# Sums of squares with the squares added on GpSimd and one ones-product on TensorE, at six places of a four-layer and expert kernel

## The chip, the core and the metric

The kernel runs on one core of a Trainium2 chip. The metric is the device time of one execution in microseconds. All arithmetic is float32. The engines are TensorE (PE in the profile, PEld for its weight loads), VectorE (DVE), ScalarE (ACT), GpSimd (POOL) and SyncE (SP), which here only issues the weight DMAs.

## What is computed

Four layers work on 256 latent tokens and 256 context tokens of 1024 features (kinds: windowed attention, low-rank attention, chunked mLSTM, windowed attention), and a further block with dilated attention, a delta rule and 32 routed experts works on the latent tokens. Around each layer's mixer stand two normalisations for each of the two token streams:

```python
def rmsnorm(x, g):
    y = xf * lax.rsqrt(jnp.mean(xf * xf, axis=-1, keepdims=True) + EPS)
    return (y * g.astype(jnp.float32)).astype(x.dtype)

h_l = rmsnorm(x_lat, g_pre) * (1.0 + sc_l[:, None, :]) + sh_l[:, None, :]
h_c = rmsnorm(x_ctx, g_pre) * (1.0 + sc_c) + sh_c
y_l, y_c = mixer(h_l, h_c, need_ctx=need_ctx)
x_lat = x_lat + gt_l[:, None, :] * rmsnorm(y_l, g_post)
if need_ctx:
    x_ctx = x_ctx + gt_c * rmsnorm(y_c, g_post)
```

The last layer (number 3) gives no context output. The sums over the 1024 features in these norms are what the change is about.

## The kernel before

Tokens lie along the free dimension and features across the 128 partitions, in KT = 8 tiles: XT holds the residual stream as 8 tiles of 512 tokens (256 latent, LATENT, then 256 context, CONTEXT), HT its normed form, YT the gated output of a mixer, SQ squares. A sum over features is a sum over 8 tiles and over partitions. `sum_squares` (L358) does both on TensorE: for each tile k it waits for the square and multiplies it by a 128x128 matrix of ones, all eight accumulating in one PSUM bank, which leaves the sum in every partition. `square` (L355) is the ScalarE square of one tile, `root` (L365) the ScalarE root of mean plus eps, `inverse` (L370) the VectorE reciprocal, `residual` (L374) the two VectorE operations per tile that scale YT and add it to XT.

The program is a row of blocks. In a block each engine runs its own list in order, engines are tied by semaphores, and at its end all engines meet at a barrier. The blocks that matter here alternate:

- `project_out` (L512), out-projection of a layer. TensorE makes 8 tiles for latent tokens (s = 0), then, in layers 0 to 2 (`beside`), 8 for context tokens (s = 1), each of 8 products of 256 columns into one of four PSUM banks. ScalarE squares each tile into SQ (L560) and copies it gated into YT (L561). VectorE adds the eight squares of the latent tiles into SQ tile 0 (`sum_tiles`, L580), and one ones-product (L528) gives the post-norm's sum. After context tile 0 comes the first root; VectorE then forms the reciprocal and the residual of the latent tokens; ScalarE squares the new residual after context tile 4; TensorE takes these squares with `sum_squares` after context tile 5, and ScalarE takes the second root after context tile 6. VectorE forms the reciprocal and then adds the squares of the context tiles (L580 again), which ends the block.
- The first block of the next layer (`window_layer` L805, `latent_layer` L912, `memory_layer` L1070). Its start is common: `first_tiles` on TensorE, `norm_scalar` on ScalarE, `norm_vector` on VectorE. TensorE makes a ones-product of the context tiles' added squares (L411), then the latent half of three tiles (j = 0, 1, 2), then `sum_squares` of the context tokens' new residual, then the latent half of tile 3 (in layers 1 and 2 also the context halves). Meanwhile ScalarE finishes the latent norm (L404), VectorE makes the context residual, 16 operations (L377, L378), and ScalarE squares each tile as it comes (L356). The sum's root and reciprocal release the context norm (L391, L404).

GpSimd is used in none of this: it runs a few memsets, one group of them in layer 2 after the context norm (L1126), and six masks of two inputs (L1908) in the later delta rule. Weights come in 2 MB chunks by DMA from SP's queue into three slots; a slot is refilled when TensorE has finished with it.

Of the kernel before, what the change touches and what calls it, by code (L numbers as in the profile page):

```python
# [14 lines left out]
KT = D // P  # L15
# [140 lines left out]
def layers_and_experts_kernel(nc, t, consts_at, out):  # L156
# [3 lines left out]
    with ctx:  # L160
# [103 lines left out]
        def modulation_chunks(l, a, b, name=None):  # L264
# [7 lines left out]
        dve_chain = Chain(ctx.enter_context(nc.semaphore("dve_chain")))  # L272
        act_chain = Chain(ctx.enter_context(nc.semaphore("act_chain")))
        pool_chain = Chain(ctx.enter_context(nc.semaphore("pool_chain")))
        names = ("vectors_loaded tokens_loaded consts_loaded late_loaded transposed transposed_taken cond_ready squares_ready "
                 "square_sum_ready rms_ready inverse_ready rstd_ready scaled_ready tile_ready tile_taken rope_mixed rope_taken "
                 "scores_ready max_ready exp_ready scores_used probs_ready probs_turned turned_copied heads_ready "
                 "heads_taken rows_copied columns_ready columns_taken h_ready normed_ready residual_ready a_ready b_ready c_ready d_ready e_ready f_ready g_ready i_ready j_ready k_ready").split()
# [2 lines left out]
        def at(name, n):  # L281
            return S[name].sem, S[name].at(n)
# [75 lines left out]
        def sum_squares(pe, tok, sums, sq):  # L358
# [3 lines left out]
                ins = nc.tensor.matmul(sums, ones, sq[:, k, tok], start=(k == 0), stop=(k == KT - 1))  # L362
            ins.then_inc(S["square_sum_ready"].sem, 1)

        def root(act, sums, tok, nth=0):  # L365

            act.wait_ge(*at("square_sum_ready", nth + 1))
            nc.scalar.activation(RMS[:, tok], sums, ACT.Sqrt, bias=const("eps"), scale=1.0 / D).then_inc(S["rms_ready"].sem, 1)
# [38 lines left out]
        def first_tiles(pe, pending, tiles, product):  # L407


            if pending:  # L410
                nc.tensor.matmul(PS[:, 6, 0:LAT], ones, SQ[:, 0, CONTEXT], start=True, stop=True).then_inc(  # L411
                    S["square_sum_ready"].sem, 1)
            for s, tok in enumerate((LATENT, CONTEXT)):
                for j, streams, done in tiles:
                    if pending and tok is LATENT and j == 3:
                        sum_squares(pe, CONTEXT, PS[:, 7, 0:LAT], SQ)
                    if s < streams:
                        for k in range(KT):
                            pe.wait_ge(*at("h_ready", s * KT + k + 1))
                            ins = product(j, k, tok)  # L420
                        if s == streams - 1:
                            ins.then_inc(done[0], 1)

        def norm_passed(streams, pending=False):
            S["normed_ready"].passed(KT * streams)
            S["h_ready"].passed(KT * streams)
            if pending:
                S["residual_ready"].passed(KT)
                S["squares_ready"].passed(KT)
                S["square_sum_ready"].passed(2)  # L430
                S["rms_ready"].passed(2)

# [79 lines left out]
        def project_out(l, ot, streams):  # L512

            first = ws.first[f"l{l}_w_out"]
            tiles = [(s, m) for s in range(streams) for m in range(KT)]
            done, n_plain = tile_signals([first + m // 4 if s == streams - 1 and m % 4 == 3 else None for s, m in tiles])
            beside = streams == 2
            with nc.Block() as block:

                @block.sync  # L520
                def _(sp):
                    ws.load_until(sp, first + 2)

                @block.tensor
                def _(pe):
                    def sum_tiles():
                        pe.wait_ge(*at("c_ready", 1))
                        nc.tensor.matmul(PS[:, 4, 0:LAT], ones, SQ[:, 0, LATENT], start=True, stop=True).then_inc(  # L528
                            S["square_sum_ready"].sem, 1)

                    for j, (s, m) in enumerate(tiles):
                        if s == 0 and m % 4 == 0:
                            ws.wait(pe, first + m // 4)
                        w = ws.view(first + m // 4)
                        if j >= 4:
                            pe.wait_ge(*at("tile_taken", j - 3))
                        for k in range(KT):
                            ins = nc.tensor.matmul(PS[:, j % 4, 0:LAT], w[:, k, (m % 4) * P:(m % 4 + 1) * P],  # L538
                                                   ot[:, k, s * LAT:(s + 1) * LAT], start=(k == 0), stop=(k == KT - 1))
                        ins.then_inc(done[j][0], 1)  # L540
                        if (s, m) == (1, 0):
                            sum_tiles()
                        if (s, m) == (1, 5):
                            sum_squares(pe, LATENT, PS[:, 5, 0:LAT], SQ)
                    if not beside:
                        sum_tiles()
                        sum_squares(pe, LATENT, PS[:, 5, 0:LAT], SQ)

                @block.scalar
                def _(act):  # L550
                    def squares():
                        for k in range(KT):
                            act.wait_ge(*at("residual_ready", k + 1))
                            square(act, k, LATENT, SQ)

                    act.wait_ge(*at("b_ready", 1))
                    for j, (s, m) in enumerate(tiles):
                        act.wait_ge(*done[j])
                        tok = slice(s * LAT, (s + 1) * LAT)
                        nc.scalar.activation(SQ[:, m, tok], PS[:, j % 4, 0:LAT], ACT.Square).then_inc(S["a_ready"].sem, 1)  # L560
                        nc.scalar.activation(YT[:, m, tok], PS[:, j % 4, 0:LAT], ACT.Copy, scale=GATE[:, m, s:s + 1]).then_inc(  # L561
                            S["tile_taken"].sem, 1)
                        if (s, m) == (1, 0):
                            root(act, PS[:, 4, 0:LAT], LATENT)
                        if (s, m) == (1, 4):
                            squares()
                        if (s, m) == (1, 6):
                            root(act, PS[:, 5, 0:LAT], LATENT, 1)
                    if not beside:
                        root(act, PS[:, 4, 0:LAT], LATENT)  # L570
                        squares()
                        root(act, PS[:, 5, 0:LAT], LATENT, 1)

                @block.vector
                def _(dve):
                    def sum_tiles(s):
                        tok = slice(s * LAT, (s + 1) * LAT)
                        for m in range(1, KT):
                            dve.wait_ge(*at("a_ready", s * KT + m + 1))
                            ins = nc.vector.tensor_tensor(SQ[:, 0, tok], SQ[:, 0, tok], SQ[:, m, tok], ALU.add)  # L580
                            if m < KT - 1:
                                dve_chain.link(dve, ins)
                        ins.then_inc(S["c_ready"].sem, 1)

                    nc.vector.tensor_tensor(GATE[:], modulation(l)[:, 2 * KT:3 * KT, :],
                                            col(f"l{l}_g_post").unsqueeze(2).to_broadcast([P, KT, 2]), ALU.mult).then_inc(S["b_ready"].sem, 1)
                    sum_tiles(0)
                    inverse(dve, LATENT)
                    dve.wait_ge(*at("tile_taken", KT))
                    residual(dve, LATENT)  # L590
                    inverse(dve, LATENT, 1)
                    if beside:
                        sum_tiles(1)

            S["tile_ready"].passed(n_plain)
            S["tile_taken"].passed(KT * streams)
            S["a_ready"].passed(KT * streams)
            S["b_ready"].passed(1)
            S["c_ready"].passed(streams)
            S["residual_ready"].passed(KT)  # L600
            S["squares_ready"].passed(KT)
            for n in ("square_sum_ready", "rms_ready"):
                S[n].passed(2)

# [200 lines left out]
        def window_layer(i, need_ctx):  # L805
# [17 lines left out]
            with nc.Block() as block:  # L823

                @block.sync
                def _(sp):
                    ws.load_until(sp, first + 5)

                @block.tensor
                def _(pe):  # L830
                    def rope(n):
# [80 lines left out]
        def latent_layer():  # L912
# [16 lines left out]
            with nc.Block() as block:  # L929

                @block.sync
                def _(sp):
                    ws.load_until(sp, c_ukv + 1)

                @block.tensor
                def _(pe):
# [133 lines left out]
        def memory_layer():  # L1070
# [46 lines left out]
            with nc.Block() as block:  # L1117

                @block.sync
                def _(sp):  # L1120
                    ws.load_until(sp, c_in + 7)

                @block.gpsimd
                def _(pool):
                    pool.wait_ge(*at("h_ready", 2 * KT))
                    nc.gpsimd.memset(raw[:, :, :, 0:2], 0.0)  # L1126
                    nc.gpsimd.memset(raw[:, :, :, LAT + 2:LAT + 4], 0.0).then_inc(S["a_ready"].sem, 1)
                    nc.gpsimd.memset(va[:, :, :, DV:DV + 1], 1.0)
# [1481 lines left out]
```

## Time and profile before

| | us |
|---|---|
| median of 3 runs | 2608.21 |
| lowest and highest | 2607.4, 2610.09 |
| span of the profiled execution | 2608.5 |
| TensorE busy in it | 2454.0 |
| VectorE busy | 921.2 |
| ScalarE busy | 640.1 |
| GpSimd busy | 15.1 |

The profiled execution has no device time of its own beside its span, which runs from its first to its last instruction; the span is 0.3 us over the median of the runs. Busy times of TensorE are modelled ends of pipelined products, so distances from start to start are used for it. A float32 product leaves two matmul records.

### The profile page before, as it was taken

Reading aid. Unit: us, or ns where it says so; the run is one execution under the profiler, and the core shown is the slowest. Engines: PE = TensorE matmul, PEld = TensorE weight load, DVE = VectorE, ACT = ScalarE, POOL = GpSimd, SP = SyncE. Lnnn points to the kernel's source line nnn. Section 1 sums busy time; section 2 is a strip of 40 time slices with the busy share of each in tenths; the row PEclk is TensorE's granted clock in tenths of the full one; section 3 lists DMA queues with packets and bytes.
Section 4 is the critical chain, followed back from the end, with each engine's and each line's share of the span. In section 5 each row is a group of like instructions: output and inputs, shape, how many; then the busy total and the mean of one; then the engine's idle time right before and its main releaser. Section 6 shows DMA issues by size and latency. Waiting matters only on the chain. (4 is left out here: it accounts for less than half of the span.)

```text
span 2608.5 us, 31940 instructions
## 1 busy us (share of the span) xinstructions
PE 2454.0 (94%) x12046; PEld 1314.0 (50%) x12047; DVE 921.2 (35%) x2118; ACT 640.1 (25%) x1479; POOL 15.1 (1%) x15
## 2 busy tenths in 40 slices
PE   6999999999999998899899789999999999999997
PEld 4546686457744567776686563333333233333222
DVE  2208523043510584427353433232232223233223
ACT  3116523232311253326332321111111111111111
POOL 0000000000000000000001000000000000000000
PEclk9999999999999998899899799999999999999999
DMA  7127920200211102238331048977999986999997
GB/s 291 65 83 273 348 93 33 81 32 1 97 65 36 63 1 76 95 120 316 137 130 65 31 187 347 415 287 293 407 418 418 418 334 270 417 418 418 418 418 296
DMA packets 154191, 568.02 MB, mean 218 GB/s; under 512 B 10800, under 2 KB 12336, under 8 KB 121040
## 3 DMA queue, kind: packets, MB, share of 16 engines
q1 hardware_dynamic: 154096, 566.72, 55.7%
q8 instruction: 63, 1.03, 0.2%
q14 instruction: 32, 0.26, 0.0%
HBM read 565.64 MB, written 1.05 MB: 217 GB/s over the span
## 5 line engine op out<-in xcount | busy, mean ns | idle before, releaser
L2335 PE MATMUL PS<-BIG,PW 128*64 128x512 f32 x2304 | 513.9, 599 | 16.7 <-DMA BIG<-in_w 16.6
L2335 PEld LDWEIGHTS PS<-BIG,PW 128*64 128x64 f32 x2304 | 159.7, 137 | 368.3 <-issue 315.9
L2359 PE MATMUL PS<-BIG,PW 128*64 128x512 f32 x1152 | 256.7, 598 | 8.6 <-ACT PW L2431 8.6
L2491 DVE TENSOR_SCALAR PW<-PS 128x512 f32<-128x512 f32 x36 | 24.9, 692 | 562.4 <-PE PS L2335 562.4
L2428 ACT ACTIVATE PW<-PW 128x512 f32<-128x512 f32 x36 | 22.7, 630 | 799.1 <-DVE PW L2491 799.1
L2359 PEld LDWEIGHTS PS<-BIG,PW 128*64 128x64 f32 x1152 | 79.5, 137 | 162.6 <-issue 145.4
L857 PE MATMUL PS<-HT,BIG 128*128 128x512 f32 (+1 forms) x448 | 155.0, 504 | 0.0
L538 PE MATMUL PS<-HT,BIG 128*128 128x256 f32 x640 | 139.5, 379 | 2.1 <-PEq L645 2.1
L538 PEld LDWEIGHTS PS<-HT,BIG 128*128 128x128 f32 x640 | 121.4, 190 | 19.1 <-issue 2.7
L857 PEld LDWEIGHTS PS<-HT,BIG 128*128 128x128 f32 x448 | 86.3, 193 | 62.9 <-issue 56.9
L1150 PE MATMUL PS<-BIG,HT 128*128 128x512 f32 x256 | 110.0, 592 | 0.0
L749 DVE TENSOR_REDUCE ST<-PS 128x2 f32<-128x1024 f32 (+2 forms) x72 | 69.9, 971 | 62.6 <-PE PS L1042 56.1
L709 ACT ACTIVATE PW<-PS,ST 128x512 f32<-128x512 f32 (+2 forms) x144 | 84.6, 591 | 19.8 <-DVE ST L757 10.5
L1150 PEld LDWEIGHTS PS<-BIG,HT 128*128 128x128 f32 x256 | 48.6, 190 | 61.2 <-issue 61.2
L723 ACT COPY PW<-PS 128x512 f32<-128x512 f32 (+2 forms) x144 | 63.3, 489 | 62.9 <-PE PS L667 62.1
L2511 DVE TENSOR_TENSOR PW<-PS,BIG 128x512 f32<-128x512 f32 x36 | 24.9, 692 | 151.6 <-PE PS L2359 151.6
L1689 PE MATMUL PS<-HT,BIG 128*128 128x256 f32 x320 | 73.1, 388 | 4.2 <-ACT HT L404 4.2
L681 PE MATMUL PS<-PW,BIG 128*64 128x128 f32 (+1 forms) x880 | 75.4, 284 | 0.0
L667 PE MATMUL PS<-CONST,PW 128*128 128x128 f32 x440 | 67.4, 292 | 6.5 <-DVE PW L770 6.4
L315 PE MATMUL PS<-BIG,COND 128*32 128x256 f32 x1152 | 70.6, 386 | 2.5 <-DVE MOD L337 2.5
L2318 PE MATMUL PS<-PW,HT 64*128 64x512 f32 x288 | 71.5, 615 | 0.9 <-DVE PW L2511 0.9
L2303 PE MATMUL PS<-BIG,HT 128*64 128x512 f32 x296 | 69.9, 593 | 2.5 <-DVE HT L2452 2.5
(433 smaller groups left out, 3189.7 us busy)
## 6 DMA issues: line engine op xcount, KB each, us to landing
BIG<-in_w SPq DMA_DIRECT2D x384, 1024.0 KB, 15.4
BIG<-in_l_w_ada SPq DMA_DIRECT2D x24, 2048.0 KB, 9.1
BIG<-in_l_w_in SPq DMA_DIRECT2D x20, 2048.0 KB, 8.0
BIG<-in_w_ada SPq DMA_DIRECT2D x12, 2048.0 KB, 8.8
BIG<-in_l_w_out SPq DMA_DIRECT2D x8, 2048.0 KB, 7.8
BIG<-in_w_in SPq DMA_DIRECT2D x7, 2048.0 KB, 8.4
BIG<-in_w_out SPq DMA_DIRECT2D x2, 2048.0 KB, 8.0
BIG<-in_l_w_in SPq DMA_DIRECT2D x1, 1792.0 KB, 11.7
```

What stands on the lines that cost most here:

```text
L315: ins = nc.tensor.matmul(PS[g:g + 32, self.bank, 0:256], COND[:, k, :], w[:, k, half * 256:half * 256 + 256], start=(k < 2), stop=(k >= KT ...
L538: ins = nc.tensor.matmul(PS[:, j % 4, 0:LAT], w[:, k, (m % 4) * P:(m % 4 + 1) * P], ot[:, k, s * LAT:(s + 1) * LAT], start=(k == 0), stop= ...
L681: ins = nc.tensor.matmul(place(heads_at(i)), lhs, turned[:, i % 2, h, j * P:(j + 1) * P], start=(j == 0), stop=(j == len(kts) - 1))
L709: nc.scalar.activation(probs[:, i % 2, h, a:b], PS[:, 2 * (i % 2) + h, a:b], ACT.Exp, bias=nm[:, i % 2, h:h + 1], scale=scale, accum_out=d ...
L749: dve_chain.link(dve, nc.vector.tensor_reduce(mx[:, i % 2, 0:2], s[:, :, a:b], AX, ALU.max))
L857: ins = nc.tensor.matmul(PS[:, j % 4, 0:tok], *ops, start=(k == 0), stop=(k == KT - 1))
L1150: ins = nc.tensor.matmul(o, HT[:, k, m[1] * P:(m[1] + 1) * P], w[:, k, :], start=(k == 0), stop=(k == KT - 1))
L1689: ins = nc.tensor.matmul(o[:, 0:LAT], w[:, k, m % 4 * P:m % 4 * P + P], HT[:, k, 0:LAT], start=(k == 0), stop=(k == KT - 1))
L2303: ins = nc.tensor.matmul(PS[64 * g:64 * g + 64, 6, :], pick[:, a, :], htok[:, a, g * 512:g * 512 + 512], start=(a == 0), stop=(a == 1))
L2318: ins = nc.tensor.matmul(PS[:, 2 * a + g, :], spread[64 * g:64 * g + 64, a * P:(a + 1) * P], ys[64 * g:64 * g + 64, :], start=False, stop= ...
L2335: ins = nc.tensor.matmul(PS[64 * g:64 * g + 64, 4 + half, :], xt[:, c % 4, c // 4, :], W[:, c, half * F + g * 512:half * F + g * 512 + 512 ...
L2359: ins = nc.tensor.matmul(PS[64 * g:64 * g + 64, 7, :], at_[:, k % 4, k // 4, :], W[:, 8 + k // 2, k % 2 * D + g * 512:k % 2 * D + g * 512 ...
```

## The change

`add_squares` is new: GpSimd waits for square k and adds it to SQ tile 0, for k = 1 to 7, each add waiting for the one before through `pool_chain`; the last one signals `squares_added`. `sum_added` is new: TensorE waits for that signal once and makes a single ones-product of SQ tile 0. They replace `sum_squares` beside the out-projections of layers 0, 1 and 2 (latent tokens) and ahead of layers 1, 2 and 3 (context tokens). In the out-projection the product moves from after context tile 5 to after context tile 6. The sums of the very first block, of layer 3's out-projection and of the second block are as before. In layer 2 the adds stand ahead of the three memsets on GpSimd.

```diff
+        def add_squares(pool, tok):
+
+            for k in range(1, KT):
+                pool.wait_ge(*at("squares_ready", k + 1))
+                ins = nc.gpsimd.tensor_tensor(SQ[:, 0, tok], SQ[:, 0, tok], SQ[:, k, tok], ALU.add)
+                if k < KT - 1:
+                    pool_chain.link(pool, ins)
+            ins.then_inc(S["squares_added"].sem, 1)
+
+        def sum_added(pe, tok, sums):
+            pe.wait_ge(*at("squares_added", 1))
+            nc.tensor.matmul(sums, ones, SQ[:, 0, tok], start=True, stop=True).then_inc(S["square_sum_ready"].sem, 1)
...
                     if pending and tok is LATENT and j == 3:
-                        sum_squares(pe, CONTEXT, PS[:, 7, 0:LAT], SQ)
+                        sum_added(pe, CONTEXT, PS[:, 7, 0:LAT])
...
+                @block.gpsimd
+                def _(pool):
+                    if beside:
+                        add_squares(pool, LATENT)
...
-                        if (s, m) == (1, 5):
-                            sum_squares(pe, LATENT, PS[:, 5, 0:LAT], SQ)
+                        if (s, m) == (1, 6):
+                            sum_added(pe, LATENT, PS[:, 5, 0:LAT])
...
+                @block.gpsimd
+                def _(pool):
+                    if pending:
+                        add_squares(pool, CONTEXT)
...
+                @block.gpsimd
+                def _(pool):
+                    add_squares(pool, CONTEXT)
...
                 @block.gpsimd
                 def _(pool):
+                    add_squares(pool, CONTEXT)
                     pool.wait_ge(*at("h_ready", 2 * KT))
```

## Rows read from the trace of the kernel before

**Rows 1.** The page: span, and busy us, share and instructions of each engine.
```profile
span 2608.5 us, 31940 instructions
PE 2454.0 (94%) x12046; PEld 1314.0 (50%) x12047; DVE 921.2 (35%) x2118; ACT 640.1 (25%) x1479; POOL 15.1 (1%) x15
```
**Rows 2.** Windows over the six sums, L362 alone: stretch, its length, busy (records), clock.
```profile
374.89:378.34 3.45, 3.45 (x16) 2.85 (x15) 1.00 0.14 51
...
1075.12:1078.57 3.45, 3.45 (x16) 2.85 (x15) 1.00 0.00 0
```
**Rows 3.** Timeline of TensorE, end of layer 0's out-projection: start, us, line, count, idle before.
```profile
374.89 3.62 PE L362 MATMUL PS<-BIG,CONST 128*128 128x256 f32 x16
378.34 7.07 PE L538 MATMUL PS<-HT,BIG 128*128 128x256 f32 x32
388.43 1.19 PE L411 MATMUL PS<-BIG,CONST 128*128 128x256 f32 x2 [3.02 <-PEq L518]
```
**Rows 4.** Timeline of ScalarE, same stretch.
```profile
372.27 2.55 ACT L356 ACTIVATE BIG<-XT 128x256 f32<-128x256 f32 x8
...
382.00 0.38 ACT L560 ACTIVATE BIG<-PS 128x256 f32<-128x256 f32 x1 [6.16 <-PE PS L538]
382.28 0.47 ACT L561 ACTIVATE BIG<-PS,GATE 128x256 f32<-128x256 f32 x1
382.63 0.48 ACT L368 ACTIVATE PW<-PS,CONST 128x256 f32<-128x256 f32 x1
```
**Rows 5.** Timeline of VectorE, same stretch; the idle time ahead is in the brackets.
```profile
383.14 1.75 DVE L372 RECIPROCAL PW<-PW 128x256 f32<-128x256 f32 x1 [14.95 <-ACT PW L368]
384.93 3.18 DVE L580 TENSOR_TENSOR BIG<-BIG 128x256 f32<-128x256 f32 x7
388.43 0.17 DVE L383 SCALAR_TENSOR_TENSOR GAIN<-MOD,COLS 128x16 f32<-128x16 f32 x1 [0.32 <-PEq L518]
```
**Rows 6.** Timeline of TensorE, start of layer 1.
```profile
390.68 12.85 PE L954 MATMUL PS<-HT,BIG 128*128 128x256 f32 x48 [1.05 <-ACT HT L404]
403.36 3.62 PE L362 MATMUL PS<-BIG,CONST 128*128 128x256 f32 x16
406.91 3.67 PE L956 MATMUL PS<-HT,BIG 128*64 128x256 f32 x32
```
**Rows 7.** Timeline of ScalarE, start of layer 1: first, second and last square, and the root.
```profile
394.02 0.42 ACT L356 ACTIVATE BIG<-XT 128x256 f32<-128x256 f32 x1
394.82 0.42 ACT L356 ACTIVATE BIG<-XT 128x256 f32<-128x256 f32 x1 [0.38 <-DVE XT L378]
...
399.59 0.42 ACT L356 ACTIVATE BIG<-XT 128x256 f32<-128x256 f32 x1 [0.38 <-DVE XT L378]
407.02 0.47 ACT L368 ACTIVATE PW<-PS,CONST 128x256 f32<-128x256 f32 x1 [7.01 <-PE PS L362]
```
**Rows 8.** Timeline of layer 3 behind its context sum.
```profile
1078.78 0.47 ACT L368 ACTIVATE PW<-PS,CONST 128x256 f32<-128x256 f32 x1 [7.12 <-PE PS L362]
...
1085.89 1.22 PE L608 MATMUL PS<-BIG,CONST 128*128 128x256 f32 x2 [3.70 <-ACT BIG L868]
```
**Rows 9.** What GpSimd runs, its wake-up after ScalarE, and the queue entries ahead of L1908.
```profile
0.71 0.31 POOL L453 MEMSET COND<- 128x256 f32 x1 [0.29 <-POOLq L2585]
696.83 0.58 ACT L404 ACTIVATE HT<-HT,MOD,GAIN 128x256 f32<-128x256 f32 x1
697.47 0.13 POOL L1126 MEMSET BIG<- 128x32 f32 x1 [696.45 <-ACT HT L404]
1398.71 2.35 POOL L1908 TENSOR_TENSOR PW<-BIG,CONST 128x1024 f32<-128x1024 f32 x1 [108.14 <-SPq L1897]
1404.19 2.36 POOL L1908 TENSOR_TENSOR PW<-BIG,CONST 128x1024 f32<-128x1024 f32 x1 [3.13 <-PE PS L1930]
L1908 POOLq MODIFY_POOL_CONFIG  x2: 11/11/11, 1398.6 to 1398.6; - x2
```
**Rows 10.** TensorE behind GpSimd's first product.
```profile
1401.21 1.62 PE L1930 MATMUL PS<-PW 128*128 128x128 f32 x10 [3.96 <-POOL PW L1908]
```
**Rows 11.** Windows over layers and experts: PE, PEld, DVE, ACT, POOL, clock, DMA share, GB/s.
```profile
325.00:1290.00 965.00, 912.51 (x4112) 609.95 (x4108) 366.11 (x997) 306.24 (x746) 0.24 (x3) 0.97 0.24 85
1560.00:2608.00 1048.00, 1007.82 (x4638) 336.58 (x4634) 311.13 (x483) 133.08 (x192) 0.00 (x0) 0.99 0.92 374
```
**Rows 12.** Windows at the start of layer 1, columns as above.
```profile
390.00:392.00 2.00, 1.32 (x3) 1.15 (x4) 2.00 (x6) 2.00 (x5) 0.00 (x0) 0.50 1.09 413
394.00:396.00 2.00, 2.00 (x8) 1.66 (x7) 1.90 (x6) 1.24 (x4) 0.00 (x0) 0.70 0.01 5
```
**Rows 13.** Timeline of VectorE, start of layer 1: first and last operations of the residual.
```profile
393.11 0.42 DVE L377 TENSOR_TENSOR BIG<-BIG,PW 128x256 f32<-128x256 f32 x1
...
399.13 0.42 DVE L378 TENSOR_TENSOR XT<-BIG,XT 128x256 f32<-128x256 f32 x1
```

## Prediction before the run

> **What bounds the kernel now.** I read the page first. TensorE is busy for 94% of the span, GpSimd for 1% [rows 1], so work taken off TensorE should be worth its time wherever TensorE, or a chain through it, ends last. Then I read each of the six places that the change edits, engine by engine. All six sums of squares look alike: eight ones-products of 256 columns, which leave 16 records (two for each float32 product), in 3.45 us at the full granted clock [rows 2]. So one product costs 3.45 / 8 = 0.431 us. Three sums lie beside an out-projection (latent tokens, layers 0, 1, 2) and three ahead of a layer (context tokens, layers 1, 2, 3). I work out one of each kind; the others have the same offsets.
>
> Beside the out-projection of layer 0, the sum runs from 374.89 to 378.34, between context tiles 5 and 6, and TensorE leaves no gap on either side; it is done with tile 7 at 385.41 and then idles for 3.02 us [rows 3]. What ends that block is another chain: tile 6 is taken by ScalarE from 382.00, the root runs at 382.63 [rows 4], then the reciprocal and seven VectorE adds, which end at 388.11, and the next block begins at 388.43 [rows 5]. The root was ready long before (its sum was finished at 378.5): it waits in ScalarE's order behind tile 6. So the path is: everything on TensorE up to the end of tile 6, then ScalarE, then VectorE.
>
> Ahead of layer 1, TensorE runs three latent tiles, reaches the sum at 403.36, leaves it, and has its next product at 406.91 [rows 6]. The squares are there from 394.44 on, the last at 400.01, and the root starts at 407.02 [rows 7]. From it hang the reciprocal, the context tokens' norm and the context tiles. Both TensorE and this chain pass through the sum. In layer 3, ScalarE has all eight norms ahead of the first tile that it takes, so TensorE waits 3.70 us until 1085.89, and this too hangs on the root at 1078.78 [rows 8].
>
> **The change part by part.**
> *Products removed.* Seven of eight at each place: 7 x 0.431 = 3.02 us off TensorE. All 3.02 are on the path at a context place if the adds are ready when TensorE comes, as root and TensorE both move.
>
> *The latent product moved behind tile 6.* Now nothing of the sum stands ahead of tile 6, so tile 6 ends 3.45 us earlier. The single product behind it ends in time: from the start of the last product to the root is 407.02 - 403.36 - 7 x 0.431 = 0.64 us [rows 6, 7], so issued at 374.89 + 3.45 = 378.34 it lets the root start at 378.98, while ScalarE, busy with tile 6, comes to it at 382.63 - 3.45 = 379.18. Tile 7 ends 3.02 earlier, at 382.4, and its square by 382.8; the seventh VectorE add would start about 384.2 (384.93 + 6 x 0.46 - 3.45), so it doesn't wait for that. The block ends up to 3.45 us earlier.
>
> *Seven GpSimd adds of 128x256, each waiting for the one before.* The trace has no such add. The nearest are the products of two 128x1024 tiles, 2.35 to 2.36 us [rows 9]. From below, a quarter of that with no fixed part: 0.59. From above: the whole 0.31 of the 128x256 memset as fixed part and the rest by size, 0.31 + (2.36 - 0.31) / 4 = 0.82. The memset of 128x32 takes 0.13 [rows 9], so with a fixed part near 0.10 the add takes 0.10 + 2.26 / 4 = 0.67. The step from one add to the next isn't in the trace: GpSimd starts 0.06 after ScalarE's end at 697.41 [rows 9], and TensorE 0.15 after GpSimd's (1401.06 to 1401.21) [rows 10]. The gap between dependent adds I bound by 0.04 and 0.15, and the pitch by 0.63 and 0.97, and take 0.80, above the middle of 0.67 + 0.10, since two unknowns add up.
>
> *Latent places at pitch p.* The squares go from 372.27 at 0.305 us each, the second is ready at 372.99 [rows 4]. The adds end at 373.04 + 7p, the root can start 0.11 + 0.64 later (a weight load follows GpSimd after 0.11), at 373.79 + 7p. The gain is 382.63 less that, at most 3.45: all 3.45 up to p = 0.77, 3.24 at 0.80, 2.05 at 0.97. VectorE rests between 368.2 and 383.14 [rows 5], so nothing disturbs the adds. Three places at 3.24: 9.7 us.
>
> *Context places at pitch p.* Squares come every 0.80 us [rows 7], about one add each; the last add can start at 400.05 and the chain from 395.3, so it ends at 395.3 + 5.6 = 400.9, or 402.1 at p = 0.97, before 403.36. Gain 3.02 each, 9.1 for three. This is what makes the context places the sturdier ones: they have 2.3 us to spare, the latent ones none.
>
> *Waits and queues.* TensorE has one wait in place of eight; behind it stand tile 7, or the last latent tile and the context tiles, so any lateness costs its full length there. On GpSimd only layer 2's memsets are queued behind the adds; they wait for the context norm, ending at 697.41, anyway. SP issues nothing new; its weight loads wait for slots that TensorE frees, so they move with TensorE. Between 325 and 1290 the DMA engines are busy 24% of the time, so the earlier start can't be met by a full queue, and the later expert stage at 92% starts from slots freed by the same path, so it shifts as a whole [rows 11]. The block ends' barrier already counts GpSimd. These cost nothing.
>
> *Sum.* 9.7 + 9.1 = 18.8 us. The profiled span is 2608.5, the median of the runs 2608.21, a difference far below this, so I take it from the median: 2589.4 us, 0.72% faster. Between the bounds of p: 19.4 (2588.8) and 3 x 2.05 + 9.1 = 15.2 (2593.0).
>
> **TensorE's clock.** The granted clock is 0.50 (1.2 GHz) from soon after a block starts until about 395.4, after TensorE had stood idle for 3 us and waited for the norm [rows 3, 12]. There the first 48 records took 12.68 us [rows 6], where 48 at the full clock take 48 x 3.45 / 16 = 10.35, so such a spell costs up to 2.3. The change shortens the idle time before it by 0.4 (TensorE's end moves 3.02, the block's 3.45), so I expect the spells to stay; shifted against the work, each of three may cost or return about 1 us. I put 3 us either way on the total.
>
> **The rivals.**
> *VectorE and GpSimd get in each other's way.* At a context place, VectorE is in an unbroken chain of 16 operations from 393.11 to 399.55, each with two inputs from SBUF [rows 13], while the adds run. No GpSimd operation in the trace ran beside such a chain, so neither side is shown. If the two alternate, each waiting for the other, five or six adds of 0.67 push the chain back by 3.7, the last square to 403.7, the last add to 404.5, the root to 405.25: the gain falls from 3.02 to 1.8. Total 9.7 + 5.3 = 15.0, or 2593.2 us. If each pass costs a hand-over on top, of 0.2 say, the context places gain 0.6 and the time is 2597. Speaking for it: both engines want two SBUF inputs at once; against: no row. The Trainium skill ("SBUF — State Buffer", section "Who interferes with whom") states that a VectorE instruction with two SBUF inputs contends with a GpSimd instruction that reads SBUF, as an exclusive lock on a shared port pair, and that the first to issue holds it; by that rule this rival is what happens, and the time is 2593.2 rather than 2589.4. No row here tests it.
>
> *The first add waits for its code.* Ahead of the first GpSimd product stand two pool-configuration entries at 1398.6, and the product starts at 1398.71 [rows 9], so nothing is waited for there, and if it were, it would fall at the block's start, 47 us before the first latent add. The Trainium skill ("GPSIMD Engine Reference", section "Instruction dispatch") gives about 6 us for the first call to a freshly loaded kernel; the row shows 0.1. Were it paid once behind the wait, the sum would be 12.8.
>
> *Slower: the pitch of dependent adds is far over the row's.* One mechanism: each add waits for the completion of the one before, and if that round trip is long, TensorE stands at its single wait. The latent gain is 8.84 - 7p, nothing from p = 1.26; the context gain 7p short of 10.98, nothing from 1.57. Together they turn at p = 1.42 and make the kernel slower by 5.2 us from p = 1.54: 2613.4. At p = 1.2 the gain is still 3 x 0.44 + 3 x 2.58 = 9.1, 2599.1 us. Against it: 1.54 is twice the row's worth.
>
> *It doesn't bring what it says.* TensorE's time is freed but given back, by longer slow-clock spells behind the shifted blocks or by weights that come later than the work. Then the time stays within 5 us. Against it: every sum was found on the path [rows 3 to 8], and the weights have room [rows 11].
>
> **How the numbers follow.** Adds beside the rest as the rows say: 0.45, 2589.4 (2586 to 2593 with p and clock). VectorE and GpSimd in each other's way: 0.35, 2593.2 (to 2597). Code wait: 0.03, 2595.4. Slow adds: 0.10, of which 0.05 between 2597 and 2603, and 0.05 slower. Given back: 0.07. The likeliest's time is the prediction. The range that leaves out no more than 2 in 10 goes from 2586 (full gains, and 3 us from the clock) to 2598. This kernel's times can be told apart at about 0.2%, 5.2 us: faster by more, 0.87; within, 0.08; slower, 0.05.
>
> **What would show it.** Right: one ones-product (2 records) at each of the six places, preceded by seven GpSimd adds at 0.7 to 0.9 us from start to start; tile 6 of layer 0's context right behind tile 5; the block's end 3.2 to 3.5 us earlier against its start; no idle time of TensorE ahead of the product at the context places; 16 VectorE operations there still in 6.45 us. Wrong: those 16 operations stretched to 9 or 10 us, or adds that take over 1 us when alone, or TensorE idle ahead of the single product with GpSimd as what it waited for.

## The result

The changed kernel takes 2591.8 us (median of 4 runs, 2588.46 to 2592.47), the kernel before beside it 2609.15. The ratio is 0.9931, with a 95% interval of 0.9920 to 0.9943: 0.7% faster, 2.4 us over the forecast time. The profiled execution has a span of 2586.7 us, and it is also the shortest of the runs (2588.46 us of device time, 1.8 over its span). By the same 1.8 us the profiled execution of the kernel before, with its span of 2608.5, would be one of about 2610.3, among the longest of its runs, so spans show a larger difference than medians.

The profile after, first the end of layer 0's out-projection (TensorE, GpSimd, ScalarE, VectorE; start, us, operation, count, idle time before). Compare it with [rows 3 to 5]:

```profile
371.76 7.93 PE L557 MATMUL PS<-HT,BIG 128*128 128x256 f32 x36
379.85 0.70 PE L376 MATMUL PS<-BIG,CONST 128*128 128x256 f32 x2 [0.15 <-POOL BIG L369]
380.39 3.62 PE L557 MATMUL PS<-HT,BIG 128*128 128x256 f32 x16
386.39 0.67 PE L424 MATMUL PS<-BIG,CONST 128*128 128x256 f32 x2 [2.38 <-PEq L532]
...
374.26 5.53 POOL L369 TENSOR_TENSOR BIG<-BIG 128x256 f32<-128x256 f32 x7 [373.24 <-ACT BIG L356]
...
373.46 2.55 ACT L356 ACTIVATE BIG<-XT 128x256 f32<-128x256 f32 x8
...
380.59 0.47 ACT L381 ACTIVATE PW<-PS,CONST 128x256 f32<-128x256 f32 x1
...
382.88 3.19 DVE L599 TENSOR_TENSOR BIG<-BIG 128x256 f32<-128x256 f32 x7
```

Tiles 5 and 6 stand together, the seven adds take 5.53 us (0.80 from one start to the next), and TensorE waits 0.15 us for the last of them. From the first square to the root it is 7.13 us, where [rows 4] have 382.63 - 372.27 = 10.36.

Then the start of layer 1, to be compared with [rows 6, 7, 13]:

```profile
392.24 8.30 PE L984 MATMUL PS<-HT,BIG 128*128 128x256 f32 x37
401.69 0.70 PE L376 MATMUL PS<-BIG,CONST 128*128 128x256 f32 x2 [1.16 <-POOL BIG L369]
...
393.27 1.72 POOL L369 TENSOR_TENSOR BIG<-BIG 128x256 f32<-128x256 f32 x2 [13.47 <-ACT BIG L356]
395.86 1.65 POOL L369 TENSOR_TENSOR BIG<-BIG 128x256 f32<-128x256 f32 x2 [0.88 <-ACT BIG L356]
398.39 1.66 POOL L369 TENSOR_TENSOR BIG<-BIG 128x256 f32<-128x256 f32 x2 [0.87 <-ACT BIG L356]
400.92 0.72 POOL L369 TENSOR_TENSOR BIG<-BIG 128x256 f32<-128x256 f32 x1 [0.87 <-ACT BIG L356]
...
393.11 0.42 DVE L391 TENSOR_TENSOR XT<-BIG,XT 128x256 f32<-128x256 f32 x1
393.45 0.95 DVE L390 TENSOR_TENSOR BIG<-BIG,PW 128x256 f32<-128x256 f32 x1
394.44 0.83 DVE L391 TENSOR_TENSOR XT<-BIG,XT 128x256 f32<-128x256 f32 x1
395.19 0.41 DVE L390 TENSOR_TENSOR BIG<-BIG,PW 128x256 f32<-128x256 f32 x1
```

Here the adds come in pairs, and beside each pair two VectorE operations take 0.95 and 0.83 us instead of 0.42. The 16 operations of the residual take 9.27 us where they took 6.45. The last add ends at 401.64, and TensorE has stood idle for 1.16 us.

The blocks, from barrier to barrier on GpSimd's queue, in the two profiled executions:

| block | before | after | difference |
|---|---|---|---|
| out-projection, layer 0 | 62.39 | 59.16 | -3.23 |
| out-projection, layer 1 | 62.40 | 59.17 | -3.23 |
| out-projection, layer 2 | 64.05 | 60.85 | -3.20 |
| first block, layer 1 | 132.89 | 130.35 | -2.54 |
| first block, layer 2 | 186.49 | 183.74 | -2.75 |
| first block, layer 3 | 103.09 | 100.24 | -2.85 |

Three latent places give 9.7 us, three context places 8.1, together 17.8; the medians differ by 17.35. The spans differ by 21.8. The 4.0 beyond are in blocks that the change doesn't touch: the expert stage is 5.1 us shorter (1047.09 to 1041.95; 1043.36 in another execution of the changed kernel), the others together 1.1 longer. The table compares two single executions. The rows of the out-projections of layers 0 and 1 came out again within 0.02 us in other executions; those of the first blocks hold slow spells of the clock that differ from one execution to the next, and the experiments show how much of the 8.1 that is.

### The profile page after: what moved, and what is told of

Same layout as the page of the kernel before. It is cut to its first block and busy times, and to the rows that moved or that the text cites. A ratio compares the mean times of both kernels' runs of the same rounds, so it can differ in the third digit from the quotient of the medians.

```text
span 2586.7 us, 31850 instructions
## 1 busy us (share of the span) xinstructions
PE 2430.8 (94%) x11962; PEld 1296.1 (50%) x11963; DVE 929.2 (36%) x2118; ACT 640.4 (25%) x1479; POOL 46.8 (2%) x57
## 3 DMA queue, kind: packets, MB, share of 16 engines
HBM read 565.64 MB, written 1.05 MB: 219 GB/s over the span
## 6 DMA issues: line engine op xcount, KB each, us to landing
BIG<-in_w SPq DMA_DIRECT2D x384, 1024.0 KB, 14.7
```

## The experiments

All ratios are to the kernel before, run on the same chip beside each, with 95% intervals. Block lengths are from the profiled execution.

**The latent places alone** (in `first_tiles` the eight products again, no adds on GpSimd in the layers' first blocks).

```diff
-                        sum_added(pe, CONTEXT, PS[:, 7, 0:LAT])
+                        sum_squares(pe, CONTEXT, PS[:, 7, 0:LAT], SQ)
...
```

> The change at the three latent places alone; ahead of the layers the eight products stay. Theory (each place is set by the latest of TensorE, the adds and ScalarE): each out-projection block of layers 0 to 2 shorter by 3.2 us, 62.4 to 59.2, as in the whole change, and the starts of the layers as before; in all 9.7 us under the kernel before. Rival (only TensorE's freed time counts): 7 products, 3.0 us in each of these blocks, 9.1 in all. Rival (part of what was gained came from the clock's spells): these blocks gain well under 3.2 once the context places are undone.

Measured: 2600.14 against 2608.89, ratio 0.9967 (0.9955 to 0.9980), 8.8 us less. The out-projection blocks of layers 0 and 1 take 59.18 us, as in the whole change: 3.2 and not 3.0, so the theory stands. Layer 2's is 59.18 too, against 64.05, and there 1.65 us are not the change's: with the latent places as before, the next kernel has 62.40 for it. The first blocks didn't stay as before, though their code is as before: layer 1's took 130.56 us (132.89 before), layer 2's 189.16 (186.49), layer 3's 100.98 (103.09). On the start of layer 1 no slow spell of the clock fell: the granted clock was 1.00 there (stretch, length, busy of PE, PEld, DVE, ACT, POOL, clock, DMA share, GB/s), and the eight products begin earlier:

```profile
386.00:396.00 10.00, 9.16 (x41) 7.13 (x42) 9.69 (x24) 7.14 (x16) 0.00 (x0) 1.00 0.41 157
...
385.12 0.67 PE L424 MATMUL PS<-BIG,CONST 128*128 128x256 f32 x2 [2.38 <-PEq L531]
386.84 11.04 PE L974 MATMUL PS<-HT,BIG 128*128 128x256 f32 x48 [1.05 <-ACT HT L417]
397.72 3.62 PE L362 MATMUL PS<-BIG,CONST 128*128 128x256 f32 x16
```

They begin 12.6 us after the block's first product, against 14.93 before [rows 3, 6]. So layer 1's block is 2.3 us shorter without the change at its context place. This matters below.

**The context places alone** (latent places with eight products behind tile 5, as before).

```diff
-                        if (s, m) == (1, 6):
-                            sum_added(pe, LATENT, PS[:, 5, 0:LAT])
+                        if (s, m) == (1, 5):
+                            sum_squares(pe, LATENT, PS[:, 5, 0:LAT], SQ)
...
```

> The change at the three context places alone. Theory (adds and VectorE's two-input operations hold each other up, and the adds' end sets the product): the ones-product starts 15.3 us after the block's start in all three layers, first blocks of layers 1 to 3 shorter by 2.5 to 2.9, in all 8 us under the kernel before. Rival (the adds are free and TensorE sets the product): it starts at 14.6 to 15.1 and the blocks are 3.0 shorter, 9.1 in all. Both theories: the out-projections as before.

Measured: 2603.48 against 2608.89, ratio 0.9981 (0.9971 to 0.9990), 5.4 us less. The product stands 15.3 us after the block's first instruction in all three layers, with TensorE idle ahead of it for 0.38, 1.37 and 1.30 us; the adds set it, not TensorE. Only layers 1 and 3 are shorter by about 2.5 (130.37, 100.59); layer 2's is at 186.42, as before, though its root came earlier, 16.06 us after the first instruction for 18.29; this block is the longest of the three and holds later slow spells, so I don't read it finer. The 8 us were too much: the product's place is fixed, but what it is compared with isn't. The old root comes 3.66 us after TensorE's arrival at the sum, the new one 16.05 us after the block's first instruction. The gain is the arrival + 3.66 - 16.05: 2.5 at 14.9, and 0.2 at 12.6, the arrival without a slow spell.

Five profiled executions have the eight products at the context places: the kernel before, the one above, and three of the kernels below. TensorE reaches them 12.6 to 15.1 us after the first instruction in layer 1 (mean 14.0), 13.9 to 15.2 in layer 2 (14.7) and 13.8 to 15.1 in layer 3 (14.1). The mean of all fifteen is 14.3, so the gain is 1.9 us a place and 5.6 in all, an estimate that agrees with the 5.4 measured. In the four of them other than the kernel before, layer 3's block took 100.98 to 101.75 us; against these the changed kernel's 100.24 is 0.7 to 1.5 us shorter, not 2.85. The medians of the two halves of the change, 8.8 and 5.4 us, add up to 14.2 where the whole gave 17.35; the intervals (about 3 us either way) allow that, and no cause is shown for it.

**Eight products, only moved behind tile 6**, without adds.

```diff
-                        if (s, m) == (1, 5):
+                        if (s, m) == (1, 6):
                             sum_squares(pe, LATENT, PS[:, 5, 0:LAT], SQ)
```

> The kernel before with the eight products of the latent places moved behind context tile 6; no GpSimd adds. Theory: tile 6 ends 3.45 us earlier but the root waits for the eight products behind it, 0.64 us after the last one's start, and the last VectorE add waits for tile 7, whose end stays; each block gains 0.6, in all 1.9 us. Rival (the move alone is what shortens the block, the adds do nothing there): 3.45 a block, 10.3 us in all.

Measured: 2604.86 against 2608.89, ratio 0.9987 (0.9978 to 0.9997), 4.0 us less, with 1.9 inside the interval. Blocks of 61.75, 61.76 and 63.45: 0.6 less in each, as the theory said. So the move is worth its 3.2 us only with a single product in place of the eight: 2.6 of them come from the two together.

**One product and GpSimd's adds, left behind tile 5** (latent places alone).

```diff
-                        if (s, m) == (1, 6):
+                        if (s, m) == (1, 5):
                             sum_added(pe, LATENT, PS[:, 5, 0:LAT])
...
```

> GpSimd adds at the latent places alone, with the single product left behind context tile 5. Theory: the adds are ready 7.2 us after tile 5's start, so TensorE idles about 3.7 us ahead of the product, tile 6 ends later than before, and each block is about 0.8 us longer, in all 2.4 us over the kernel before. Rival (seven products off TensorE are worth their time wherever the one stands): 3.0 us less a block, 9 us less in all.

Measured: 2615.14 against 2608.89, ratio 1.0023 (1.0013 to 1.0033), 6.3 us more. TensorE in layer 0, then two stretches with the granted clock (columns as above):

```profile
378.58 1.22 PE L376 MATMUL PS<-BIG,CONST 128*128 128x256 f32 x2 [3.62 <-POOL BIG L369]
379.60 9.54 PE L556 MATMUL PS<-HT,BIG 128*128 128x256 f32 x32
...
374.89:378.58 3.69, 0.08 (x1) 0.00 (x0) 0.00 (x0) 0.75 (x2) 3.33 (x5) 0.89 0.12 44
378.58:385.47 6.89, 6.89 (x18) 5.62 (x19) 0.00 (x0) 0.00 (x0) 0.00 (x0) 0.56 0.00 0
```

The idle time is the 3.7 us expected, but the size was wrong: the blocks are 3.8, 3.5 and 2.6 us longer, not 0.8. After the idle time the clock was at 1.2 GHz for most of tile 6: its eight products leave 16 records, with the ones-product 18, and these took 6.9 us where the full clock takes 3.9. Those 3.0 us are what layer 0's block exceeds the 0.8 by. Freed time of TensorE is worth nothing if the one product left makes it wait.

**Each add in two halves** of 128 columns (latent places alone).

```diff
-                ins = nc.gpsimd.tensor_tensor(SQ[:, 0, tok], SQ[:, 0, tok], SQ[:, k, tok], ALU.add)
...
+                for x in (slice(0, P), slice(P, 2 * P)):
+                    ins = nc.gpsimd.tensor_tensor(SQ[:, 0, x], SQ[:, 0, x], SQ[:, k, x], ALU.add)
...
```

> The latent places alone, each add in two of 128 columns, so 14 dependent adds. By the measured adds (0.722 at 256 columns, 2.357 at 1024) one of 128 takes 0.45, with 0.08 to the next, so a pitch of 1.06 for each tile. Theory (gain of a place = 8.84 - 7 x pitch, at most 3.45): 1.4 us a block, 61.0 instead of 59.2, in all 4.2 us under the kernel before; the root stands by 1.8 later than with whole adds. Rival (ScalarE's order or tile 7 sets the block, the adds have room): the blocks stay within 0.5 of 59.2.

Measured: 2598.13 against 2607.17, ratio 0.9965 (0.9951 to 0.9978), 9.0 us less. The 4.2 lie outside the interval (5.7 to 12.8), so by the total the expectation failed, and this kernel can't be told apart from the one with whole adds. By the blocks it can: 61.57, 61.02 and 62.69 against 62.39, 62.40 and 64.05 before, so 0.8, 1.4 and 1.4 less, where whole adds gave 3.2. The fourteen adds:

```profile
373.00 7.37 POOL L370 TENSOR_TENSOR BIG<-BIG 128x128 f32<-128x128 f32 x14 [371.98 <-ACT BIG L356]
...
380.43 0.70 PE L377 MATMUL PS<-BIG,CONST 128*128 128x256 f32 x2 [2.00 <-POOL BIG L370]
380.97 5.30 PE L557 MATMUL PS<-HT,BIG 128*128 128x256 f32 x16
```

A pitch of 7.37 / 7 = 1.05 a tile, as expected, and in two of three blocks the gain of 1.4 that 8.84 - 7p gives. TensorE idled 2.0 us ahead of the product in all three. In layer 0 tile 7 then ran at a slow clock (5.30 us for 3.62), which puts its square, and with it the block's end, later: 0.6 of the gain is gone. In layers 1 and 2 it took 3.62. So the formula holds in the blocks; the lower total is from blocks without the change (layer 1's first block, whose sum TensorE reached after 12.61, is 2.3 us shorter, the expert stage 3.7), and I show no cause for it.

**The scale in PSUM.** VectorE's first operation per tile then has one input from SBUF, one from PSUM.

```diff
-                    inverse(dve, CONTEXT)
-                    residual(dve, CONTEXT)
+                    inverse(dve, CONTEXT, out=PS[:, 5, 0:LAT])
+                    residual(dve, CONTEXT, PS[:, 5, 0:LAT])
...
```

> The changed kernel, but ahead of the layers the reciprocal of the context tokens' scale is written to a PSUM bank, so the first of VectorE's two operations per tile reads one input from SBUF and one from PSUM; the second still reads two from SBUF. Theory (an add and a VectorE operation with two SBUF inputs exclude each other): the first operation stays at 0.42 us beside an add, against 0.95 in the changed kernel, the second is still held up to about 0.8; the chain of 16 takes 7.6 to 8.5 us instead of 9.27 and the product stands at 14.2 to 14.9 after the block's start instead of 15.4, unless TensorE comes later. Rival (any VectorE operation that touches SBUF is held up): both stay at 0.8 to 0.95, and the product at 15.4.

Measured: 2583.58 against 2607.17, ratio 0.9905 (0.9889 to 0.9920). Start of layer 1, GpSimd, VectorE, TensorE:

```profile
392.92 6.02 POOL L369 TENSOR_TENSOR BIG<-BIG 128x256 f32<-128x256 f32 x7 [13.47 <-ACT BIG L356]
...
393.10 0.41 DVE L391 TENSOR_TENSOR BIG<-BIG,PS 128x256 f32<-128x256 f32 x1
393.55 0.51 DVE L392 TENSOR_TENSOR XT<-BIG,XT 128x256 f32<-128x256 f32 x1
393.98 0.41 DVE L391 TENSOR_TENSOR BIG<-BIG,PS 128x256 f32<-128x256 f32 x1
...
400.02 0.59 PE L376 MATMUL PS<-BIG,CONST 128*128 128x256 f32 x2
```

The operation that reads PSUM takes 0.41 us wholly inside an add (393.10 to 393.51, the add runs from 392.92 to about 393.77), where it took 0.95 with two inputs from SBUF. The other kind, still with two, comes to the same add late and is held for only 0.09: it ends at 394.06, 0.28 us after the add. The chain of 16 is 6.82 us long, better than the 7.6 to 8.5 of the theory, the adds end at 12.9, and the product stands where TensorE comes: 13.99, 13.93 and 15.0 after the block's first instruction. In these operations VectorE is held up only where it wants a second input from SBUF. The Trainium skill ("SBUF — State Buffer", "Who interferes with whom") says that a VectorE instruction with two SBUF inputs contends with a GpSimd instruction that reads SBUF, that one with at most one doesn't outside certain modes, and that the contention is an exclusive lock. The traces agree: in the changed kernel too the held operation ends at 394.40, 0.28 after its add (393.27 + 0.85 = 394.12), and the one with one SBUF input isn't held.

**The adds only after all eight squares.**

```diff
-                pool.wait_ge(*at("squares_ready", k + 1))
+                pool.wait_ge(*at("squares_ready", KT if tok is CONTEXT else k + 1))
```

> The changed kernel, but at the context places GpSimd starts only when all eight squares are there, when VectorE has nothing to do. Theory (the two hold each other up only where they overlap): VectorE's 16 operations are back at 0.42 and 6.45 us, the adds at 0.72; the adds end 17.2 us after the block's start, the product at 17.3, TensorE idles 2 to 4 us ahead of it and may fall to the slow clock; each of the three blocks is 1.9 us or more longer than in the changed kernel, in all 2597 to 2602. Rival (the adds are slower there for another reason, such as TensorE's or ScalarE's traffic): they stay at 0.79.

Measured: 2598.1 against 2607.17, ratio 0.9962 (0.9949 to 0.9975). Start of layer 1, GpSimd and TensorE:

```profile
396.35 5.53 POOL L369 TENSOR_TENSOR BIG<-BIG 128x256 f32<-128x256 f32 x7 [18.25 <-ACT BIG L356]
401.93 1.22 PE L376 MATMUL PS<-BIG,CONST 128*128 128x256 f32 x2 [4.47 <-POOL BIG L369]
403.08 5.31 PE L986 MATMUL PS<-HT,BIG 128*64 128x256 f32 x24
```

Seven adds again take 5.53 us, as at the latent places, where TensorE was busy beside them, and the residual is back at 6.45. So it is the overlap with VectorE that slowed both. To overlap still pays: apart, the adds end 1.9 us later, and layer 1's block is 4.6 us longer than in the changed kernel and layer 2's 3.3, each with a slow spell of the clock behind the stall. Layer 3's took 100.11, no more than the changed kernel's 100.24; there the clock fell for a shorter time behind the stall, and a slow spell is missing that the kernel before and the changed one have over 20 us into the block. The total is in the expected 2597 to 2602.

**All adds on VectorE**, no GpSimd.

```diff
             for k in range(KT):
+                if tok is CONTEXT and k >= 3:
+                    add_square(dve, CONTEXT, k - 2)
...
```

(the last two behind the residual, and all seven ahead of the second reciprocal at the latent places).

> No GpSimd at either kind of place: VectorE makes all the adds, at the latent places while it waits for the second root, at the context places between its residual operations. Theory: at 0.46 a step the latent adds are there before tile 6 ends, so the root is set by ScalarE alone and the out-projection blocks are 3.45 us shorter than before (58.95) instead of 3.23; at the context places the chain of 23 operations takes about 8.7 us without holding or being held, the product stands at 14.3 after the block's start or where TensorE comes later (14.6 to 15.2), against 15.4. In all 1 to 2.5 us under the changed kernel, 2589.3 to 2590.8. Rival (VectorE becomes the bound at the context places, GpSimd is what makes the change pay): product at 16 or later, and the kernel slower than the changed one by 1 to 3 us.

Measured: 2589.21 against 2607.17, ratio 0.9932 (0.9919 to 0.9946). The out-projections take 58.94, 58.95 and 60.63, so 3.45 less than the first two were before. Start of layer 1, VectorE's first operation of the chain and the last two adds, then TensorE's product:

```profile
390.48 0.42 DVE L400 TENSOR_TENSOR BIG<-BIG,PW 128x256 f32<-128x256 f32 x1
...
399.14 0.42 DVE L376 TENSOR_TENSOR BIG<-BIG 128x256 f32<-128x256 f32 x1
399.78 0.42 DVE L376 TENSOR_TENSOR BIG<-BIG 128x256 f32<-128x256 f32 x1 [0.22 <-ACT BIG L356]
...
400.70 0.59 PE L384 MATMUL PS<-BIG,CONST 128*128 128x256 f32 x2
```

The chain of 23 operations takes 400.20 - 390.48 = 9.72 us in all three layers, not the 8.7 of the theory, and no operation in it is held. The product stands at 14.9, 14.5 and 14.5 after the block's first instruction. In layer 1 TensorE comes last; in layers 2 and 3 it waits 0.4 and 0.6 us for VectorE's last add, still 0.85 earlier than the changed kernel's product. The total is level with the changed kernel's ratio, so the 1 to 2.5 us are not shown by the time.

**Adds on VectorE at the latent places, scale in PSUM at the context places**, with the changed kernel on the same chip.

> Latent places with the adds on VectorE, as in the kernel without GpSimd adds; context places with the adds on GpSimd and the scale in PSUM. Theory: each kind of place is now set by something other than its adds: the out-projection blocks take 58.94 us (3.45 less than before) instead of 59.17, the product of the context places stands where TensorE comes, 13.9 to 15.1 after the block's start, with no idle time ahead of it. In all 0.7 us under the kernel with the scale in PSUM alone, 6 to 8 us under the changed kernel, about 0.990 of the kernel before. Rival (the gain of the scale in PSUM was mostly the clock's luck): within 3 us of the changed kernel sent with it.

> The changed kernel once more, on the same chip as the one above. All theories: about 0.993 of the kernel before; out-projection blocks of 59.17 us, products of the context places 15.4 us after the block's start, whatever the clock's spells do; the blocks between may differ by 1.7 us each with those spells.

Measured: 2585.95 (0.9908, 0.9893 to 0.9923) and 2589.13 (0.9923, 0.9909 to 0.9936) against 2609.45. The blocks did as said: 58.95, 58.95 and 60.64 against 59.17, 59.17 and 60.86; products at 13.9 to 15.1 against 15.3. The gain over the changed kernel is 3.2 us, not 6 to 8, and the intervals overlap. So part of the 7 us that the scale in PSUM seemed to bring over the changed kernel, across two chips' comparisons, was not its own. By the profiled executions the six blocks with the change are 2.5 us shorter than in the changed kernel on the same chip, and 2.9 with the scale in PSUM alone. That is what the blocks show; by the times, that either is faster than the changed kernel is likely and not shown.

## Why the prediction came out as it did

- **What bounds it**: right. The latent path through tile 6, root, reciprocal and seven adds gave 3.23 us where 3.24 was worked out, and moving alone gave 0.6, the single product left where it was a loss.
- **The add's price**: 0.80 taken, 0.80 measured. It has other parts than assumed: 0.722 for the add (0.67 expected) and 0.08 to the next (0.13 expected). The 0.80 was a choice between the bounds 0.63 and 0.97, and the two errors cancel, so that 3.23 agrees with 3.24 is in part luck.
- **The context places**: the likeliest case failed. That they are "the sturdier ones" and "have 2.3 us to spare" counted squares coming every 0.80 us, and that pace was VectorE's alone. Two of the signs that the prediction named for being wrong came: the 16 operations at 9.27 us, and TensorE idle ahead of the single product with GpSimd as what it waited for. The rival of the two engines in each other's way is what happened. Its size was off: not five or six adds of 0.67 in VectorE's way but six operations held by 0.53 and 0.41 in turn, 2.8 us instead of 3.7, so the root stands at 16.05 after the block's start instead of 16.8. The block gains were 2.5 to 2.9, against 3.02 in the likeliest case and 1.8 in the rival, and the time, 2591.8, lies between their 2589.4 and 2593.2. That it lies within 2.4 us of the forecast doesn't bear the likeliest case out.
- **What the context sum was worth**: right for that execution, too sure in general. The gain was taken against an arrival of TensorE that held a slow spell of the clock. Without one it is 0.2 us; over five executions the estimate is 1.9 a place instead of the 3.02.
- **The clock**: spells stayed, and 3 us either way was the right order: the 4.0 us in untouched blocks of the profiled execution are more than the error of the sum. What was missing is that a stall in mid-block can be followed by the slow clock: after one of 3.6 us this cost 3.0 us more, nearly the stall again.
- **Code wait**: none. Two pool-configuration entries stand at 327.2, at the block's start, and the first add at 374.26 takes 0.73, like the others.
- **Slow adds, gains given back**: neither; the adds follow each other at 0.80, and 17.35 us were gained.

## What to carry to other kernels

Work taken from a busy engine is worth what the latest of three arrivals allows: the engine, the helper that took the work, and whoever uses the result; here the one product left had to stand one tile later, or waiting for GpSimd's adds turned the change into a loss. Before giving GpSimd adds beside VectorE, look at where VectorE's inputs lie: an operation with one of its two in PSUM wasn't held here. The adds could also stay on VectorE where it has time, with no difference that the times show. And compare by blocks, with the clock beside them, and over several executions, when the runs scatter by as much as the change brings.

## What the runs showed of the hardware

- A GpSimd add of two SBUF tiles takes 0.45 us at 128 columns, 0.72 at 256 (0.79 beside VectorE), and the product of the same kind 2.36 at 1024; the next dependent one starts 0.08 later.
- A VectorE operation of 0.42 us with two SBUF inputs takes up to 0.95 beside such an add, and 0.41 if one input is in PSUM. The held one ends 0.28 us after the add, whether it came early or late.
- TensorE idle for 3.6 us in mid-block was followed by a granted clock of 1.2 GHz in most of the next 6.9 us; idle for 1.16 us it kept 2.4 GHz. Idle for 2.0 us (each add in two halves) it fell in one of three blocks, idle for 2.1 us (adds after all squares, layers 2 and 3) it fell in both (mean 0.75 in the 6.8 us from the product on).
